# An eighteenth weight slot, taken from GpSimd's descriptor scratch, and a turned ring in layer 1

## The chip, the cores and the metric

The kernel runs on one core of one Trainium2 chip. The metric is the device time of one execution in microseconds, as the median of several runs. TensorE multiplies (its weight loads are listed apart as PEld), VectorE (DVE), ScalarE (ACT) and GpSimd (POOL) do the rest, and SyncE (SP) issues nearly all weight loads. Sixteen DMA engines move the data between memory and the on-chip rows of 128 partitions. They are fed by three queues that matter here: q1 is SyncE's, q10 is ScalarE's, q0 is GpSimd's, whose descriptors GpSimd writes by itself into a scratch area in each partition.

## What is computed

One step of a two-layer encoder trunk on 512 new frames and 32 further frames of a running stream, model width 1024, all in float32.

```python
for i in range(DEPTH):                       # two layers
    hp_n = rms_norm(hp, norm_mix[i]); hs_n = rms_norm(hs, norm_mix[i])
    if i % N_MIXERS == 0:                    # layer 0: sliding window attention, 16 heads, 4 kv heads
        yp, kp_, vp_ = mixer_a_prompt(hp_n, w_a_qkv[j], b_a_qkv[j], a_sinks[j], w_a_o[j])
    else:                                    # layer 1: differential attention, 8 heads
        yp, kp_, vp_ = mixer_b_prompt(hp_n, w_b_qkv[j], b_lambda[j], b_subln[j], w_b_o[j], lam_init)
    hp = hp + yp
    hp = hp + hier_moe(rms_norm(hp, norm_ffn[i]), ...)
y_prompt = rms_norm(hp, norm_final)

# hier_moe: top-1 of 4 groups, then top-2 of its 8 experts
a = jnp.einsum('nd,edf->nef', x, w_gate[g])
u = jnp.einsum('nd,edf->nef', x, w_up[g])
hh = jax.nn.silu(a) * u * gate[:, g, :, None]
y = y + jnp.einsum('nef,efd->nd', hh, w_down[g])
```

Each expert has three matrices (gate, up, down) of 1 MB each, and there are 32 experts in each layer, so an expert stage reads 96 MB.

## The kernel before

The program goes through four stages: mixer A, the expert stage of layer 0, mixer B, the expert stage of layer 1. Frames lie in five tiles, four of 128 rows and one of 32 (tile 4).

**Weights and slots.** Every weight is loaded in pieces of 1 MB, one piece to a slot of 2048 floats in each partition (`SLOT`). There are 17 slots for the expert weights, and they are named after what else lies there: R0 to R5 are the ring for the mixers' weights (`A_RING`, `B_RING`, lines 172 and 173), F0 to F6 hold keys, values, tables and the transposed input during attention, N0 and N1 the rows of the norm, X0 and X1 the router's input. `MOE_SLOTS` (line 175) lists them in the order in which the expert weights take them, round and round. `weight_loads` gives each weight its slot, and the loop under it notes who held it before (`BEFORE`).

**The order on SyncE.** SyncE issues all loads in the order of their use: the 10 of mixer A, 96 of layer 0's experts, 16 of mixer B (q, k and v of four pairs of heads, then the four pieces of the output matrix), 96 of layer 1's experts. Before each, `load_after_owner` (line 475) waits until the last user of what the slot held is done. The first turn of the expert weights waits with `vacant` for the attention's data instead. As the queue is in order, a load whose slot is not free holds up all that follow it.

**Overfull experts.** An expert takes up to 64 rows (`CAP`). If one has more, its weights are loaded once more after expert 29 (`OV_AFTER`), into three slots side by side (`ovw`), which the numbering of the stream leaves out (`expert_stream`). With these inputs that happens once, in layer 1 (line 488).

**One expert.** GpSimd gathers its rows (line 611), TensorE turns them (L1955), multiplies by gate and up (L1970, L1971), ScalarE and VectorE make the product, TensorE turns it (L1976) and multiplies by down (L1982, L1983), VectorE copies the result (L1407), GpSimd scatters it to a scratch tensor in memory (L617). When all scatters of a layer have landed, ScalarE's queue reads them back tile by tile (L927, semaphores `tile_in`), VectorE adds them to the residual (L1506, L1507), and the next norm begins.

**Space.** `area` is one array that fills the partition beside a few small ones. GpSimd's scratch for descriptors has the program's default size of 16384 bytes a partition.

Of the kernel before, what the change touches and what calls it, by code (L numbers as in the profile page):

```python
# [31 lines left out]
NT = 5  # L32
# [23 lines left out]
SLOT = 2048  # L56
XG = 4
OV_AFTER = 29
# [88 lines left out]
def out_items(layer):  # L147
# [10 lines left out]
    if layer == 0:  # L158
# [9 lines left out]
            for layer in range(2)]  # L168
# [1 line left out]


A_RING = ["R0", "R1", "R2", "R3", "R4", "R5"]
B_RING = ["R4", "R5", "R0", "R1", "R2", "R3"]
FREED = ["F5", "F6", "F0", "F1", "F2", "F3", "F4"]
MOE_SLOTS = [["R4", "R5"] + FREED + ["R0", "R1", "R2", "R3", "N0", "N1", "X0", "X1"],
             ["R2", "R3"] + FREED + ["R4", "R5", "R0", "R1", "N0", "N1", "X0", "X1"]]
NSLOT = len(MOE_SLOTS[0])


def expert_stream(e, j):  # L180
    return 3 * (e + (e > OV_AFTER)) + j


def weight_loads():
    loads = [("a", x, i) for x, n in (("k", 1), ("v", 1), ("q", 4), ("o", 4)) for i in range(n)]
    loads = [(key, A_RING[i % 6]) for i, key in enumerate(loads)]
    moe = [[(("e", layer, e, j), MOE_SLOTS[layer][expert_stream(e, j) % NSLOT]) for e in range(NE) for j in range(3)]
           for layer in range(2)]
    b = [("b", x, p) for p in range(PAIRS) for x in "kvq"] + [("b", "o", s) for s in range(4)]
    b = [(key, B_RING[i % 6]) for i, key in enumerate(b)]  # L190
    return loads, moe, b


A_LOADS, MOE_LOADS, B_LOADS = weight_loads()
WHERE, BEFORE = {}, {}
turns, owner = {}, {}
for weight, slot_name in A_LOADS + MOE_LOADS[0] + B_LOADS + MOE_LOADS[1]:
# [1 line left out]
    WHERE[weight] = slot_name, 16 * turns[slot_name]  # L199
    BEFORE[weight] = owner.get(slot_name)  # L200
    owner[slot_name] = weight
assert [MOE_SLOTS[layer][(3 * (OV_AFTER + 1) + j) % NSLOT] for layer in range(2) for j in range(3)] == ["F1", "F2", "F3"] * 2


def build(nc, I, O):
    ctx = ExitStack()
    with ctx:
        program(nc, ctx, I, O)


def program(nc, ctx, I, O):
    def sb(name, shape, dt=F32):
        return ctx.enter_context(nc.sbuf_tensor(name, shape, dt))

    def sem(name):
        return ctx.enter_context(nc.semaphore(name))
# [13 lines left out]
    R_X = M0 + 3248  # L230
    R_N = R_X + KD * N
    R_R = R_N + 4 * D
    R_F = R_R + 6 * SLOT
    AREA = R_F + 5 * SLOT + KD * N
    area = sb("area", [P, AREA])

    def part(at, *shape):
        n = int(np.prod(shape))
        v = area[:, at:at + n]
        if len(shape) == 2:  # L240
            v = v.rearrange("p (a b) -> p a b", b=shape[1])
        if len(shape) == 3:
            v = v.rearrange("p (a b c) -> p a b c", b=shape[1], c=shape[2])
        return v

    slot_at = {f"R{i}": R_R + SLOT * i for i in range(6)}
    slot_at.update({f"F{i}": R_F + SLOT * i for i in range(7)})
    slot_at.update({f"N{i}": R_N + SLOT * i for i in range(2)})
    slot_at.update({f"X{i}": R_X + SLOT * i for i in range(2)})


    oT = part(R_X, KD, N)
    xTn = [part(R_F + 5 * SLOT, KD, N), oT, part(R_F + 5 * SLOT, KD, N), oT]

# [7 lines left out]
    dist_a = part(R_X + 3328, 2 * P)  # L262
    kTa = part(R_F, A_KV, SEQ + WINDOW + DEC)
    tabA = part(R_F + A_KV * (SEQ + WINDOW + DEC), A_HEADS, 2 * P)
    R_VA = R_F + A_KV * (SEQ + WINDOW + DEC) + A_HEADS * 2 * P
    va = part(R_VA, 6, AKV)
# [29 lines left out]
    hts = [part(M1 + 1536 + 128 * i, 2, CAP) for i in range(2)]  # L296
    yout = [part(M1 + 1792 + 512 * i, OUT_HALF) for i in range(3)]
    assert M1 + 1792 + 3 * 512 <= M0
    ovw = part(R_F + SLOT, 3, SLOT)
    y2b = [part(2 * D * i, 2, D) for i in range(3)] + [part(R_X + 2 * D * i, 2, D) for i in range(2)]  # L300
    assert 6 * D <= M0 and 4 * D <= KD * N

# [39 lines left out]
    tile_in = [sem(f"tile_in{i}") for i in range(NT)]  # L342
# [11 lines left out]
    hid_moe = sem("hid_moe")  # L354
    k_out = sem("k_out")
    kb_out, vb_out = [sem(f"kb_out{i}") for i in range(2)], [sem(f"vb_out{i}") for i in range(2)]
    pool_own, dve_own, act_own = sem("pool_own"), sem("dve_own"), sem("act_own")
    q_mm, q_act, q_dve = sem("q_mm"), sem("q_act"), sem("q_dve")
    kv_mm, kv_sb, k_flip, k_sb = sem("kv_mm"), sem("kv_sb"), sem("k_flip"), sem("k_sb")
    pos_mm, pos_dve, pos_act = sem("pos_mm"), sem("pos_dve"), sem("pos_act")  # L360
# [27 lines left out]
    def wait_apart(eng, s, value):  # L388

        eng.wait_ge(s, value)  # L390
        eng.sem_inc(passed, 1)

    def weights(key):
        name, value = WHERE[key]
        return part(slot_at[name], SLOT), w_ready[name], value

    def last_use(key):

        kind, x, i = key[0], key[1], key[2]
        if kind == "e":  # L400
            return (d_mm if key[3] == 2 else gu_mm), NE * x + i + 1
        if x == "o":
            return o_mm, OUT_BASE["ab".index(kind) + 1]
        if kind == "a":
            return (q_mm, 4 * i + 4) if x == "q" else (kv_mm, NT)
        reads = {"k": "K KS", "v": "V KS", "q": "Q"}[x].split()
        return pos_mm, 1 + max(n for n, s in enumerate(POS) if s.pair == i and s.main in reads)
# [41 lines left out]
    @block.sync  # L449
    def _(sp):  # L450
        def rows8(w, lo, hi):
            return w[:, lo:hi].rearrange("(p k) f -> p k f", k=KD)

        def rows128(w, lo, hi):
            return w[:, lo:hi].rearrange("(k p) f -> p k f", p=P)

        gate = [I["w_gate"][l].rearrange("g e (p k) f -> (g e) p k f", k=KD) for l in range(2)]
        up = [I["w_up"][l].rearrange("g e (p k) f -> (g e) p k f", k=KD) for l in range(2)]
        down = [I["w_down"][l].rearrange("g e (c p) d -> (g e) p c d", p=P) for l in range(2)]

        def source(key):
            kind, x, i = key[0], key[1], key[2]
            if kind == "e":
                return (gate, up, down)[key[3]][x][i]
            if x == "o":
                return rows128(I[f"w_{kind}_o"][0], F * i, F * i + F)
            at_col = {"aq": 0, "ak": AQ, "av": AQ + AKV, "bq": 0, "bk": D, "bv": 2 * D}[kind + x] + F * i
            return rows8(I[f"w_{kind}_qkv"][0], at_col, at_col + F)

        def load(key):  # L470
            dst, landed, _ = weights(key)
            src = source(key)
            sp.dma_start(dst.rearrange("p (k f) -> p k f", f=src.shape[-1]), src).then_inc(landed, 16)  # L473

        def load_after_owner(key):
            if BEFORE[key] is not None:
                sp.wait_ge(*last_use(BEFORE[key]))
            load(key)

        def moe_loads(layer):  # L480
            s = ov[layer]

            def overfull_weights(o):
                wait_apart(sp, s["pick"], o + 1)
                e = sp.value_load(ov_u[0:1, 0:1], min_val=0, max_val=NE - 1)
                for j, w in enumerate((gate, up, down)):
                    src = w[layer][bass.ds(e, 1)].rearrange("o p k f -> p (o k) f")
                    sp.dma_start(ovw[:, j, :].rearrange("p (k f) -> p k f", f=src.shape[-1]), src) \
                      .then_inc(s["w"], 16)

            for n, (key, name) in enumerate(MOE_LOADS[layer]):
                if key[2:] == (OV_AFTER + 1, 0):
                    for j in range(3):
                        e, w = divmod(expert_stream(OV_AFTER + 1, 0) - 3 + j - NSLOT, 3)
                        sp.wait_ge(*last_use(("e", layer, e, w)))
                    sp.wait_ge(s["count"], 1)
                    extra = sp.value_load(ov_i[0:1, layer:layer + 1], min_val=0, max_val=MAX_EXTRA)
                    with sp.If(extra > 0):
                        overfull_weights(0)
                free = vacant(layer, name) if expert_stream(*key[2:]) < NSLOT else None  # L500
                if free is None:
                    load_after_owner(key)
                else:
                    for signal in free:
                        sp.wait_ge(*signal)
                    load(key)

            with sp.If(extra > 1):
                with sp.Fori(1, extra) as o:
                    overfull_weights(o)  # L510

        for n, (key, name) in enumerate(A_LOADS):
            if n == 0:
                sp.wait_ge(tile_in[0], 16)
            if n == 2:
                sp.wait_ge(tile_in[2], 16)
            load_after_owner(key)
        moe_loads(0)
        for key, name in B_LOADS:
            load_after_owner(key)  # L520
        moe_loads(1)

# [250 lines left out]

    @block.scalar
    def _(act):
        own = Link(act_own)

        def square(n, i):
            t = TILES[n][i]
            r = ROWS[t]  # L780
# [90 lines left out]
        for step in range(UNITS):  # L871
# [3 lines left out]
            j, i = divmod(step, NT)  # L875
# [1384 lines left out]
```

## Time and profile before

| | us |
|---|---|
| median of 3 runs | 1256.02 |
| lowest and highest | 1254.98, 1256.83 |
| the profiled execution | 1257.34 |
| its span, first to last instruction | 1255.6 |

| Engine | busy us | share |
|---|---|---|
| TensorE matmul | 1060.9 | 84% |
| TensorE weight load | 754.9 | 60% |
| VectorE | 419.2 | 33% |
| ScalarE | 220.3 | 18% |
| GpSimd | 282.6 | 23% |

The mean granted clock of TensorE is 0.932. The stages stand in time like this: mixer A until about 250 us, the experts of layer 0 until 536, mixer B from 558 to about 920, the experts of layer 1 until 1214, and then the last norm and the outputs. A busy share over the whole span hides this: what a change in a stage is worth is read from that stage's own waits.

### The profile page before, as it was taken

To read this page: it belongs to the slowest core of one execution; us is meant where nothing else is said; L and a number is where in the kernel's file an instruction comes from. 1 tells how busy PE (TensorE), PEld (TensorE's weight loads), DVE (VectorE), ACT (ScalarE), POOL (GpSimd) and SP (SyncE) were. 2 spreads that over 40 slices of the span, in tenths; PEclk is the share of its full clock that TensorE was granted. 3 is DMA by queue.
4 is the path that set the end of the run, shared out by engine and by line. 5 is a ranking of instruction groups with operands and counts; after the bars stand their busy time and mean duration, and the time that the engine had idled before them with its cause. 6 is when DMAs were issued, how large, how long until landed. Compare 5 with 4: busy or idle time off the path is not lost.

```text
span 1255.6 us, 17940 instructions
## 1 busy us (share of the span) xinstructions
PE 1060.9 (84%) x6864; PEld 754.9 (60%) x6864; DVE 419.2 (33%) x1340; ACT 220.3 (18%) x687; POOL 282.6 (23%) x445
## 2 busy tenths in 40 slices
PE   5999999949988887819999999999959997888850
PEld 4877778935545544518677686867845554554520
DVE  2234554322222222243243424345542322321225
ACT  2134442110000000011123322323310000000001
POOL 2512231012321212131021222221211222222113
PEclk9999999969999999959999999999969999898885
DMA  9211124199999999980322203060378999999943
GB/s 313 71 63 34 54 83 189 38 334 342 371 380 382 388 381 373 346 308 15 102 77 79 67 29 117 27 252 1 122 271 311 379 374 383 375 384 382 387 155 148
DMA packets 81239, 279.00 MB, mean 222 GB/s; under 512 B 10958, under 2 KB 37662, under 8 KB 63424
## 3 DMA queue, kind: packets, MB, share of 16 engines
q1 hardware_dynamic: 63440, 231.75, 50.1%
q0 software_dynamic: 15840, 34.92, 8.6%
q10 hardware_dynamic: 1872, 11.14, 2.4%
q8 instruction: 58, 0.95, 0.3%
q14 instruction: 29, 0.24, 0.1%
HBM read 265.50 MB, written 28.70 MB: 234 GB/s over the span
## 4 chain that ended last, share of the span: by engine, by line
PE 61%; DMA 26%; SPq 3%; DVE 3%; issue 2%; ACT 2%; POOL 1%; POOLq 0%; ACTq 0%; DVEq 0%
PE ps L1689 20%; DMA area<-in_w_up 18%; PE ps L1970 11%; PE ps L1681 10%; PE ps L1982 4%; SPq L473 3%; PE ps L1955 2%; DMA area<-in_w_down 2%; PE ps L1697 2%; PE ps L2162 2%; DMA hn_scratch<-area 1%; PE ps L1853 1%; PE ps L2128 1%; DMA area<-hn_scratch,idx_i 1%; PE ps L1868 1%
## 5 line engine op out<-in xcount | busy, mean ns | idle before, releaser
L1970 PE MATMUL ps<-area 128*64 128x256 f32 x1040 | 265.2, 413 | 60.4 <-DMA area<-in_w_up 52.6
L1689 PE MATMUL ps<-area 128*128 128x256 f32 x1152 | 267.0, 385 | 5.6 <-DMA area<-in_w_a_qkv 3.1
L1971 PE MATMUL ps<-area 128*64 128x256 f32 x1040 | 265.9, 414 | 0.0
L1689 PEld LDWEIGHTS ps<-area 128*128 128x128 f32 x1152 | 215.8, 192 | 36.7 <-issue 8.0
L1970 PEld LDWEIGHTS ps<-area 128*64 128x64 f32 x1040 | 149.7, 149 | 134.9 <-issue 76.9
L617 POOL DMA_INDIRECT y_scratch<-area,idx_i x64 | 64.8, 1013 | 401.7 <-DVE area L1407 396.9
L1971 PEld LDWEIGHTS ps<-area 128*64 128x64 f32 x1040 | 149.6, 149 | 0.0
L1982 PE MATMUL ps<-area 128*64 128x512 f32 x260 | 125.4, 604 | 1.1 <-DVE area L1400 0.8
L1983 PE MATMUL ps<-area 128*64 128x512 f32 x260 | 125.4, 604 | 0.0
L1681 PE MATMUL ps<-area 128*128 128x272 f32 x512 | 123.2, 395 | 0.0
L1392 DVE TENSOR_TENSOR area<-area,ps 64x256 f32<-64x256 f32 x64 | 27.2, 425 | 283.0 <-ACT area L903 283.0
L903 ACT ACTIVATE area<-ps 64x256 f32<-64x256 f32 x64 | 24.1, 376 | 508.6 <-PE ps L1971 508.6
L1681 PEld LDWEIGHTS ps<-area 128*128 128x128 f32 x512 | 95.0, 190 | 18.9 <-issue 0.6
L865 ACT ACTIVATE area<-area,small 128x256 f32<-128x256 f32 (+5 forms) x160 | 80.2, 502 | 87.1 <-DVE small L1157 87.1
L1955 PEld LDWEIGHTS ps<-cst,area 64*128 64x128 f32 x512 | 61.3, 200 | 45.6 <-issue 34.5
L1955 PE MATMUL ps<-cst,area 64*128 64x64 f32 x512 | 70.2, 278 | 21.5 <-DMA area<-hn_scratch,idx_i 21.5
L1150 DVE CUSTOM_DVE_ANT_0 area<-ps,area 128x256 f32<-128x256 f32 (+5 forms) x160 | 59.1, 423 | 44.9 <-PE ps L1853 25.2
L611 POOL DMA_INDIRECT area<-hn_scratch,idx_i x64 | 60.8, 949 | 47.9 <-issue 29.4
L729 POOL TENSOR_SCALAR area<-area,small 32x288 f32<-32x288 f32 (+4 forms) x40 | 20.6, 524 | 166.3 <-DVE small L1577 166.3
L1982 PEld LDWEIGHTS ps<-area 128*64 128x64 f32 x260 | 30.4, 136 | 42.9 <-issue 37.1
L1386 DVE TENSOR_TENSOR area<-ps,gT 128x512 f32<-128x512 f32 x65 | 44.9, 691 | 31.7 <-PE ps L1955 28.3
L602 POOL TENSOR_SCALAR area<-area,small 128x256 f32<-128x256 f32 (+2 forms) x80 | 33.9, 442 | 93.9 <-DVE small L1185 93.9
(218 smaller groups left out, 1059.0 us busy)
## 6 DMA issues: line engine op xcount, KB each, us to landing
area<-in_w_gate SPq DMA_DIRECT2D x65, 1024.0 KB, 26.9
area<-in_w_up SPq DMA_DIRECT2D x65, 1024.0 KB, 26.5
area<-in_w_down SPq DMA_DIRECT2D x65, 1024.0 KB, 26.8
area<-in_w_b_qkv SPq DMA_DIRECT2D x12, 1024.0 KB, 9.6
area<-y_scratch ACTq DMA_DIRECT2D x8, 1024.0 KB, 10.5
area<-in_w_a_qkv SPq DMA_DIRECT2D x6, 1024.0 KB, 13.2
out<-area POOLq DMA_DIRECT2D x12, 512.0 KB, 3.5
area<-in_w_a_o SPq DMA_DIRECT2D x4, 1024.0 KB, 5.3
```

Source lines behind the costliest of these rows:

```text
L611: nc.gpsimd.indirect_dma_start(xg[e % XG][0:CAP, :], None, hn_dram, bass.IndirectOffsetOnAxis(ap=idx_i[0:CAP, 1, e:e + 1], axis=0), bounds ...
L617: nc.gpsimd.indirect_dma_start(y2_dram, bass.IndirectOffsetOnAxis(ap=idx_i[:, 0, e:e + 1], axis=0), yout[e % 2], None, bounds_check=4 * N ...
L865: ins = nc.scalar.activation(E[:r, g, 0:nk], E[:r, g, 0:nk], ACT.Exp, bias=sm[:r, 4 + g:5 + g], scale=SCALE, accum_out=sm[:r, 8 + g:9 + g])
L1150: ins = nc.vector.tensor_tensor_reduce(out=E[:r, g, 0:nk], in0=ps[:r, b, c:c + nk], in1=tab(j, g)[:r, tc:tc + nk], scale=1.0, scalar=-3e38 ...
L1386: return nc.vector.tensor_tensor(x, ps[:, bank, :].rearrange("p (k c) -> p k c", c=CAP), gT[:, layer, :].unsqueeze(2).broadcast_to([P, KD, ...
L1681: ins = nc.tensor.matmul(ps[:, bank, 0:HALF_N], w[:, k, m * P:m * P + P], x[:, k, HALF_N * h:HALF_N * h + HALF_N], start=k == 0, stop=k == ...
L1689: ins = nc.tensor.matmul(ps[:r, bank, at_col:at_col + F], x[:, k, COL[t]:COL[t] + r], w[:, k, :], start=k == k0, stop=k == k1 - 1)
L1955: ins = nc.tensor.transpose(ps[:, 2 + b, k * CAP:k * CAP + CAP], x[:, k, :], ident[0:CAP, 0:CAP])
L1970: nc.tensor.matmul(ps[0:CAP, bank, 0:F], x[:, k, :], wg[:, k, :], start=k == 0, stop=k == KD - 1)
L1971: ins = nc.tensor.matmul(ps[CAP:P, bank, 0:F], x[:, k, :], wu[:, k, :], start=k == 0, stop=k == KD - 1)
L1982: nc.tensor.matmul(ps[0:CAP, bank, :], ht[:, c, :], wd[:, c, 0:OUT_HALF], start=c == 0, stop=c == 1)
L1983: ins = nc.tensor.matmul(ps[CAP:P, bank, :], ht[:, c, :], wd[:, c, OUT_HALF:D], start=c == 0, stop=c == 1)
```

## The change

1. The program is made with a scratch of 4096 bytes a partition for GpSimd's descriptors in place of 16384. Of the 12288 bytes, `area` takes 8192 for one further slot, S0, right behind R5.
2. S0 becomes the third entry of the list of slots, which now has 18 entries and is the same for both layers. The order of mixer B's ring changes so that it begins with R0.
3. The overfull expert's weights go to R4, R5 and S0 in place of F1, F2 and F3.
4. Before the fifth load of mixer B, SyncE waits until the y rows of the last tile of layer 0 have landed (`tile_in[NT - 1]` at 32).
5. A semaphore and a helper of ScalarE that nothing used are left out.

```diff
 A_RING = ["R0", "R1", "R2", "R3", "R4", "R5"]
-B_RING = ["R4", "R5", "R0", "R1", "R2", "R3"]
+B_RING = ["R0", "R1", "R2", "R3", "R4", "R5"]
 FREED = ["F5", "F6", "F0", "F1", "F2", "F3", "F4"]
-MOE_SLOTS = [["R4", "R5"] + FREED + ["R0", "R1", "R2", "R3", "N0", "N1", "X0", "X1"],
-             ["R2", "R3"] + FREED + ["R4", "R5", "R0", "R1", "N0", "N1", "X0", "X1"]]
+MOE_SLOTS = [["R4", "R5", "S0"] + FREED + ["R0", "R1", "R2", "R3", "N0", "N1", "X0", "X1"]] * 2
...
-    R_F = R_R + 6 * SLOT
+    R_S = R_R + 6 * SLOT
+    R_F = R_S + SLOT
...
+    slot_at["S0"] = R_S
...
-    ovw = part(R_F + SLOT, 3, SLOT)
+    ovw = part(R_R + 4 * SLOT, 3, SLOT)
...
-        for key, name in B_LOADS:
+        for n, (key, name) in enumerate(B_LOADS):
+            if n == 4:
+                sp.wait_ge(tile_in[NT - 1], 32)
             load_after_owner(key)
...
-    nc = bacc.Bacc("TRN2", target_bir_lowering=False, num_devices=1)
+    nc = bacc.Bacc("TRN2", target_bir_lowering=False, num_devices=1, dynamic_dma_scratch_size=4096)
```

## Rows read from the trace of the kernel before

**Rows 1.** The page, part 2: busy tenths of the DMA engines in 40 slices

```profile
DMA  9211124199999999980322203060378999999943
```

**Rows 2.** Sums by stretch: stretch, length, engines' busy us, clock, DMA share, GB/s

```profile
280.00:290.00 10.00, 9.82 (x78) 5.92 (x80) 2.33 (x6) 0.38 (x1) 1.03 (x1) 1.00 0.71 264
...
350.00:530.00 180.00, 147.78 (x1010) 90.58 (x1008) 40.07 (x80) 7.52 (x20) 38.02 (x39) 0.93 1.01 376
...
1040.00:1190.00 150.00, 124.27 (x822) 74.93 (x819) 37.98 (x92) 6.02 (x16) 30.45 (x32) 0.89 1.02 383
```

**Rows 3.** Waits of TensorE, 272 to 540 us: total us, times, longest

```profile
PE ps L1970 <- DMA area<-in_w_up: 32.2, 18, 3.5
```

**Rows 4.** Waits of TensorE, 938 to 1216 us

```profile
PE ps L1970 <- DMA area<-in_w_up: 20.4, 10, 4.4
...
PE ps L1970 <- DMA area<-in_w_down: 1.5, 1, 1.5
```

**Rows 5.** The page, part 6: DMA issues, KB each, us from issue to landing

```profile
area<-in_w_gate SPq DMA_DIRECT2D x65, 1024.0 KB, 26.9
...
area<-in_w_b_qkv SPq DMA_DIRECT2D x12, 1024.0 KB, 9.6
```

**Rows 6.** Timeline of SyncE before the experts of layer 0: start, us, what

```profile
154.79 0.41 SPq L473 DMA_DIRECT2D area<-in_w_gate  x1
204.08 0.33 SPq L473 DMA_DIRECT2D area<-in_w_up  x1
...
249.55 0.33 SPq L473 DMA_DIRECT2D area<-in_w_gate  x1
...
278.42 0.38 SPq L473 DMA_DIRECT2D area<-in_w_down  x1
```

**Rows 7.** Timeline of SyncE before the experts of layer 1

```profile
822.02 0.88 SPq L473 DMA_DIRECT2D area<-in_w_gate  x1
830.87 0.33 SPq L473 DMA_DIRECT2D area<-in_w_up  x1
```

**Rows 8.** The chain that ended last, end of layer 1: start, us, what

```profile
1160.87 26.97 DMA area<-in_w_down
...
1214.38 2.71 DMA y_scratch<-area,idx_i
1217.17 6.01 DMA area<-y_scratch
```

**Rows 9.** Timeline of TensorE: the expert before the overfull one; idle before, and releaser

```profile
1175.26 0.40 PE L1970 MATMUL ps<-area 128*64 128x256 f32 x1 [0.72 <-DMA area<-in_w_up]
```

**Rows 10.** Timeline of SyncE, end of layer 0

```profile
508.22 30.49 SPq L473 DMA_DIRECT2D area<-in_w_b_qkv  x6
```

**Rows 11.** The chain that ended last, end of layer 0

```profile
536.56 6.26 DMA y_scratch<-area,idx_i
...
542.91 8.35 DMA area<-y_scratch
```

**Rows 12.** DMA queues, 543 to 552 us: packets, MB, share of 16 engines

```profile
q10 hardware_dynamic: 235, 1.79, 49.0%
...
q1 hardware_dynamic: 605, 0.62, 21.2%
```

**Rows 13.** Line 473 from 501.5 us on: the last expert weight of layer 0

```profile
L473 SPq DMA_DIRECT2D area<-in_w_down x1: 6536/6536/6536, 501.5 to 501.5; - x1
...
DMA to landing us min/median/max: 27.9/27.9/27.9
```

**Rows 14.** Timeline of TensorE: its first products for head pair 1

```profile
618.49 3.72 PE L1689 MATMUL ps<-area 128*128 128x256 f32 x16
```

**Rows 15.** Line 617, all scatters: ns min/median/max, first and last start

```profile
L617 POOL DMA_INDIRECT y_scratch<-area,idx_i x64: 982/1015/1034, 288.8 to 1214.4; - x64
...
DMA to landing us min/median/max: 2.3/7.1/8.5
```

**Rows 16.** Timeline of GpSimd, end of layer 0, last of seven

```profile
540.29 0.63 POOL L683 DMA_DIRECT2D area<-in_dist_b  x1
```

More of the change, by code:

```diff
@@ L201 @@
     owner[slot_name] = weight
-assert [MOE_SLOTS[layer][(3 * (OV_AFTER + 1) + j) % NSLOT] for layer in range(2) for j in range(3)] == ["F1", "F2", "F3"] * 2
+assert [MOE_SLOTS[layer][(3 * (OV_AFTER + 1) + j) % NSLOT] for layer in range(2) for j in range(3)] == ["R4", "R5", "S0"] * 2
 def build(nc, I, O):
@@ L356, in program @@
     kb_out, vb_out = [sem(f"kb_out{i}") for i in range(2)], [sem(f"vb_out{i}") for i in range(2)]
-    pool_own, dve_own, act_own = sem("pool_own"), sem("dve_own"), sem("act_own")
+    pool_own, dve_own = sem("pool_own"), sem("dve_own")
     q_mm, q_act, q_dve = sem("q_mm"), sem("q_act"), sem("q_dve")
@@ L775, in _ @@
     def _(act):
-        own = Link(act_own)
         def square(n, i):
```

## The prediction

> **What bounds the kernel now.** I read the page's second part first, for which slices are held by which resource, then the sums by stretch, then who waited for whom on TensorE, then the chain at the end of each layer's expert stage, and last SyncE's own timeline, because SyncE issues every weight load in a fixed order. In the slices the reader is to see two long runs in which the DMA line stands at 9 [rows 1]: these are the two expert stages. By stretch, the DMA share is 1.01 and 1.02 at 376 and 383 GB/s from 350 to 530 us and from 1040 to 1190 us, while TensorE is busy for 148 of 180 and 124 of 150 us [rows 2]. TensorE's idle time there is put down to weights that had not landed: 32.2 us in 18 waits in layer 0 [rows 3], 20.4 us in 10 waits in layer 1 and another 1.5 us on the overfull expert's down weight [rows 4]. So both expert stages end when the stream of weights ends. A load counts 1024 KB, and from issue to landing it takes 26.9 us at the median [rows 5]; so some ten loads stand queued, and SyncE runs far ahead of TensorE. Before each of these stages there is plenty of DMA time with nothing in it (the 0s and 2s of the DMA line), because all slots that are free are full. What matters for the end of a stage is how many bytes have landed when the stream becomes unbroken.
>
> **The eighteenth slot, layer 0.** Loads now start as slots fall free, in batches: R4 first, then three up to 154.79 (R5, F5, F6), five from 204.08 (F0 to F4), four from 249.55 (R0 to R3), four when the norm's and the router's rows are out (N0 to X1), and the first reuse at 278.42 [rows 6], which has the last of the second batch and the first of each later one. With S0 third in the list, the batch at 154 has four loads (R5, S0, F5, F6), and every later batch has as many as before, at the same times, because the same events free the same slots. Each is one load further on in the stream. The added load follows 154.79, some 50 us before the next batch, and finds a 1 and a 2 in the DMA line [rows 1]. The stall after it does not go: from 280 to 290 us the DMA share is 0.71 [rows 2], since R4, R5 and then the next slots wait for TensorE's first two experts (278.42 is the first), and those are not earlier. From there the stream is unbroken to its end, and it has one load less to bring: 1.049 MB at 376 GB/s is **2.8 us**. Ends: 0, if TensorE came to be the bound, and 2.8. I take 2.8, since the waits that would have to be used up first are 32.2 us.
>
> **Layer 1.** The same count: four loads up to 822.02 (R2, R3, F5, F6) become five (R4, R5, S0, F5, F6), and the three from 830.87 are as before [rows 7]. The ring order of mixer B is only turned, so that each of its weights still takes the slot of the weight six before it, and R4, R5 are now the ones that its last two hold. The stream ends earlier by 1.049 MB at 383 GB/s, **2.7 us**. Here the end is tighter. The chain passes the overfull expert's down weight, which lands at 1160.87 + 26.97 = 1187.84 [rows 8], and TensorE waited for that for 1.5 us only [rows 4]. But the expert ahead of it itself began at 1175.26 on a landing [rows 9], so it moves with the stream. Ends 0 and 2.7; I take 2.7.
>
> **Between the layers.** The overfull weights move from F1 to F3 to R4, R5 and S0, so the new code gives mixer B's first four loads R0 to R3 and holds the fifth and sixth (v and q of head pair 1) until the last y rows of layer 0 are in. Before, six loads go out in the 30.49 us from 508.22, until 538.7 [rows 10], beside the last scatter and the y rows. What this costs is seen by setting the two ends side by side: from the issue of the last scatter to the landing of the first y rows it is 6.26 + 8.35 us plus the issue in layer 0 [rows 11] and 2.71 + 6.01 us in layer 1, where no such loads run [rows 8]. The difference, 5.9 us, is what all traffic beside it costs. While the first y rows were under way (543 to 552 us), SyncE's queue moved 0.62 MB beside 1.79 MB of ACT's [rows 12]. In the new order the stream and its four loads end earlier: the last expert weight lands at about 526.6 (issued at 501.5, landed 27.9 later [rows 13], less 2.8), the four loads follow at about 3 us each, so until 539, against a scatter issued at 533.8 (536.56 less 2.8). So the scatter gains about 1 us of its 3.6 us excess, and the y rows the 0.62 MB, at 385 GB/s 1.6 us, together **2.5 us**. Ends: 0 and 5.9.
> The Trainium skill (DMA: Bandwidth & Descriptors, Queues, rings and completion order) says that each DMA engine takes turns between its queues packet by packet. ACT's packets are 7.6 KB and SyncE's 1.0 KB here (bytes by packets), so by that rule SyncE's two loads would take an eighth as much as the y rows, 0.2 MB or 0.6 us, and the sum would be 1 us smaller (1249.0 us, between the forecast and rival B). The trace has 0.62 MB against 1.79 MB, a third, and I go by that.
>
> **The wait added on SyncE** (on the y rows of tile 4) has queued behind it v and q of pair 1, then k, v and q of pair 2. The y rows of tile 4 are in soon after the first ones (551.3 less 2.8 and 2.5), by about 557, and mixer B's weights land after 9.6 us at the median [rows 5], so v and q are there by some 570. TensorE reaches pair 1's k at 618.49 [rows 14], and v and q only after that; k of pair 2 has to wait for the last use of pair 0's k in both kernels, which is later than 557. A cover of some 50 us; cost nothing. The unused link of ScalarE and the shifted addresses are no instructions.
>
> **The smaller scratch.** GpSimd issues 64 gathers and 64 scatters of 1.0 us each, which land after 7.1 us at the median and 8.5 at most (scatters [rows 15]). One scatter and one gather go per expert of some 8 us, so two to four are in flight, and the densest stretch (two scatters and five loads, the last at 540.29 [rows 16]) has at most eight. The durations from the first to the last scatter, 0.982 to 1.034 us, do not grow with what has gone before. No row shows a full ring. Bounds: nothing, and a wait for the landing of the DMA before, 7.1 us for each of about seven issues on the chain. I take nothing, as a quarter of the space for at most eight DMAs is nearer to the rows than a wait for the previous one.
> The skill gives the scratch as 16 KiB a partition (SBUF: State Buffer, SBUF size: 192, 224, or 256?) and nine 16-byte descriptors per engine for a 1 MiB transfer (DMA: Bandwidth & Descriptors, The descriptor swizzle). An estimate from both is 256 descriptors or 28 such transfers in what is left. No run here shows that number.
>
> **The sum.** 2.8 + 2.5 + 2.7 = 8.0 us. The profiled execution took 1257.34 us (span 1255.6 and 1.7 around it), so it would be 1249.3; it lies 1.3 over the median of 1256.02, so the median becomes **1248.0 us**.
>
> **Rivals.**
> *A, layer 1 keeps its end.* The overfull expert needs a gather as well, and TensorE's mean clock is down to 0.89 there [rows 2], so its own chain may end the stage. For it: only 1.5 us of wait on the last weight [rows 4]. Against: expert 29 began on a landing. 2.8 + 2.5 gives 1250.7. 0.17.
> *B, no relief between the layers.* The scatter and y rows are slowed by GpSimd's own five loads [rows 16], which stay, and only the streams gain: 5.5 us, 1250.5. For it: 0.62 MB is little in 9 us. 0.15; a relief of half the size (1249.2) lies between B and the forecast, and in the forecast's chance.
> *C, full relief.* The whole 5.9 us goes: 11.4 us, 1244.6. Against: four loads still run into the scatter. 0.06.
> *D, slower: the descriptor ring fills.* Its place is GpSimd's issue. On the chain are the last row write and first gather and the last scatter of each layer and the last output, seven issues. The gain of 8.0 us is gone from 1.14 us more for each, that is if an issue of 1.0 us becomes one of 2.1. With two more us for each it is +14 - 8 = +6, 1262. In the expert loop it would have to pass (8 - 2)/2 = 3 us an issue before GpSimd paces the stage; a wait for the landing before would do it, 2 x 8.1 us an expert against 8, and cost hundreds of us. 0.06.
> *E, it does not do what it says.* The added load lands early, but the DMA stall at 280 and 950 us grows by as much, so the streams end as now, and the relief is small: within 2.5 us of 1256. For it: SyncE's order is fixed. Against: no event that frees a slot moves later. 0.06.
>
> **Chances and range.** The forecast has 0.50. 0.2% is 2.5 us, about what a measurement of this kernel can tell from no change: faster by more than that 0.87 (forecast, A to C, less 0.01), same 0.07, slower 0.06. The range takes in C, A and B with their spread and leaves out D and E: 1244.3 to 1252.8.
>
> **What would show it.** After: the batch before 160 us has one load more; the stall near 285 us stays; the last landing of layer 0's stream and the last scatter (now 536.56) come 2.5 to 3 us earlier; from last scatter to first combine 12 us in place of 14.7; mixer B the same length; layer 1's last scatter (1214.38) 8 us earlier; the weight waits on TensorE less by about 2.8 us each; GpSimd's issues at 1.015 us. Wrong: a scatter issue above 1.1 us, TensorE waiting for v or q of pair 1, or a layer's weight waits unchanged.

## The result and the profile after

| | before | changed |
|---|---|---|
| median of 4 runs, us | 1256.22 | 1241.22 |
| lowest and highest | 1254.98, 1256.83 | 1240.47, 1244.46 |
| the profiled execution | 1257.34 | 1244.46 |
| its span | 1255.6 | 1242.7 |
| granted clock of TensorE | 0.932 | 0.935 |

The ratio is 0.9882, with a 95% interval from 0.9868 to 0.9896, so the change takes off 14.8 us (13.1 to 16.6). A later set of six runs gave 1242.80 against 1256.42, ratio 0.9899 (0.9882 to 0.9915), 12.7 us less (10.7 to 14.8). Fast executions alone count here and below: one of the eight of the kernel with all but the slot took 2654.79 us and is left out. I had predicted 1248.0, in a range from 1244.3 to 1252.8: the direction was right, the gain was nearly twice the forecast and lay outside the range.

Line numbers of the new kernel are one higher (L1971 is L1970 of before), GpSimd's gather L614 and its scatter L620. First, SyncE's timeline (start, us, engine line op, tiles): the second batch, which has four loads now, and what follows the batch at 248 us.

```profile
152.19 0.34 SPq L474 DMA_DIRECT2D area<-in_w_up  x1
152.57 0.43 SPq L474 DMA_DIRECT2D area<-in_w_down  x1
153.12 0.40 SPq L474 DMA_DIRECT2D area<-in_w_gate  x1
153.62 0.71 SPq L474 DMA_DIRECT2D area<-in_w_up  x1
...
247.89 0.33 SPq L474 DMA_DIRECT2D area<-in_w_up  x1
...
261.33 0.38 SPq L474 DMA_DIRECT2D area<-in_w_down  x1
...
279.45 0.33 SPq L474 DMA_DIRECT2D area<-in_w_gate  x1
```

The added load is there, in a batch that is over long before the next one. But the first reuse comes 31.56 us after the batch at 248 us (279.45 - 247.89), where it came 28.87 us after it before (278.42 - 249.55, [rows 6]). Most of that difference is between executions: over all profiles the reuse comes 30.1 us after the batch at the mean of seven with 17 slots (28.9 to 30.9) and 30.9 at the mean of five with 18 (29.5 to 31.6). So the stall stayed, as I had said, and by these means it grew by some 0.8 us. The sum of the stretch from 280 to 290 us (columns as in [rows 2]) shows it in the changed kernel, with a share of 0.65 and 228 GB/s against 0.71 and 264:

```profile
280.00:290.00 10.00, 9.46 (x76) 5.73 (x77) 3.18 (x7) 0.38 (x1) 0.13 (x1) 1.00 0.65 228
```

TensorE's waits on weights from 272 to 540 us (total, times, longest), against 32.2 in [rows 3]:

```profile
PE ps L1971 <- DMA area<-in_w_up: 29.2, 17, 4.2
```

and from 938 to 1216 us, against 20.4 and 1.5 in [rows 4]:

```profile
PE ps L1971 <- DMA area<-in_w_up: 19.3, 10, 4.0
...
PE ps L1971 <- DMA area<-in_w_down: 1.6, 1, 1.6
```

The chain that ended last (start, us, what), first at the end of layer 0, then at the end of layer 1 and at the very end:

```profile
534.17 5.22 DMA y_scratch<-area,idx_i
...
539.47 7.28 DMA area<-y_scratch
```

```profile
1208.43 2.82 DMA y_scratch<-area,idx_i
1211.34 6.00 DMA area<-y_scratch
...
1238.44 0.52 POOL out L549
```

From the last scatter's issue to the landing of the first y rows it is 12.6 us (534.17 to 546.75) where it was 14.7 in [rows 11]. Layer 1's last scatter is 5.95 us earlier than in [rows 8] (1208.43 against 1214.38), and the last piece of the chain stands 5.9 us earlier too. Yet the span is 12.9 us shorter. Some 7 us therefore went after everything that the chain of waits shows. The view of the program's last line has them (op, times, ns min/median/max, first and last start). Of before, where it was there to be read:

```profile
L207 DVEq DRAIN  x1: 1303/1303/1303, 1242.7 to 1242.7; - x1
...
L207 POOLq DRAIN  x1: 8650/8650/8650, 1246.7 to 1246.7; - x1
...
L207 SPq EVENT_SEMAPHORE  x1: 17/17/17, 1255.5 to 1255.5; - x1
```

and of the changed kernel:

```profile
L206 POOLq DRAIN  x1: 1627/1627/1627, 1240.8 to 1240.8; - x1
```

Near the end of each engine's part of the program stands an instruction DRAIN, and SyncE's last instruction comes behind the longest of them. VectorE's takes 1.3 us and is over before GpSimd's begins. GpSimd's took 8.65 us at the end of the path in the kernel before, and 1.63 us in the changed one: **7.0 us**. It is not spent on data under way: in every profile the last output has landed 0.2 us before this drain begins (1246.50 and 1246.68 in the kernel before, 1240.64 and 1240.82 in the changed one). No work of GpSimd had been taken away, only space; it issues 198 DMAs in both kernels. The experiments ask if this is so, and where the rest came from.

### The profile page after: what moved, and what is told of

Its sections match the earlier page's. It is cut to its first block, busy times and chain, and to the rows that moved or that the text cites. A ratio compares the mean times of both kernels' runs of the same rounds, so it can differ in the third digit from the quotient of the medians.

```text
span 1242.7 us, 17941 instructions
## 1 busy us (share of the span) xinstructions
PE 1061.1 (85%) x6864; PEld 756.9 (61%) x6864; DVE 419.0 (34%) x1340; ACT 220.1 (18%) x687; POOL 281.5 (23%) x445
## 4 chain that ended last, share of the span: by engine, by line
PE 63%; DMA 24%; SPq 5%; DVE 3%; issue 2%; ACT 2%; POOL 1%; POOLq 0%; ACTq 0%; DVEq 0%
PE ps L1690 20%; DMA area<-in_w_up 16%; PE ps L1971 11%; PE ps L1682 10%; PE ps L1983 4%; SPq L474 4%; PE ps L1956 2%; DMA area<-in_w_down 2%; PE ps L1698 2%; PE ps L2163 2%; DMA hn_scratch<-area 2%; DMA area<-hn_scratch,idx_i 1%; PE ps L1854 1%; PE ps L2129 1%; PE ps L1869 1%
## 5 line engine op out<-in xcount | busy, mean ns | idle before, releaser
L1971 PE MATMUL ps<-area 128*64 128x256 f32 x1040 | 265.1, 413 | 56.2 <-DMA area<-in_w_up 48.5
L1971 PEld LDWEIGHTS ps<-area 128*64 128x64 f32 x1040 | 149.6, 149 | 129.8 <-issue 68.0
L620 POOL DMA_INDIRECT y_scratch<-area,idx_i x64 | 64.7, 1010 | 398.2 <-DVE area L1408 362.1
L1151 DVE CUSTOM_DVE_ANT_0 area<-ps,area 128x256 f32<-128x256 f32 (+5 forms) x160 | 59.1, 423 | 44.9 <-PE ps L1854 25.2
L614 POOL DMA_INDIRECT area<-hn_scratch,idx_i x64 | 60.6, 947 | 49.7 <-issue 30.3
L732 POOL TENSOR_SCALAR area<-area,small 32x288 f32<-32x288 f32 (+4 forms) x40 | 20.5, 521 | 166.4 <-DVE small L1578 166.4
L1387 DVE TENSOR_TENSOR area<-ps,gT 128x512 f32<-128x512 f32 x65 | 44.9, 691 | 33.2 <-PE ps L1956 30.1
## 6 DMA issues: line engine op xcount, KB each, us to landing
area<-in_w_a_qkv SPq DMA_DIRECT2D x6, 1024.0 KB, 13.1
```

Source lines behind the costliest of these rows:

```text
L614: nc.gpsimd.indirect_dma_start(xg[e % XG][0:CAP, :], None, hn_dram, bass.IndirectOffsetOnAxis(ap=idx_i[0:CAP, 1, e:e + 1], axis=0), bounds ...
L620: nc.gpsimd.indirect_dma_start(y2_dram, bass.IndirectOffsetOnAxis(ap=idx_i[:, 0, e:e + 1], axis=0), yout[e % 2], None, bounds_check=4 * N ...
L1151: ins = nc.vector.tensor_tensor_reduce(out=E[:r, g, 0:nk], in0=ps[:r, b, c:c + nk], in1=tab(j, g)[:r, tc:tc + nk], scale=1.0, scalar=-3e38 ...
L1971: nc.tensor.matmul(ps[0:CAP, bank, 0:F], x[:, k, :], wg[:, k, :], start=k == 0, stop=k == KD - 1)
```

## The experiments

Theory R (reclaiming): the drain's length hangs on the scratch, alone worth 7 us. Its rival T: the space isn't the cause, and the whole gain comes from the slot and the hold. The parts were tried one at a time.

**The scratch alone.** The kernel before with

```diff
+    nc = bacc.Bacc("TRN2", target_bir_lowering=False, num_devices=1, dynamic_dma_scratch_size=4096)
```

> The kernel before with 4096 bytes of scratch in place of 16384, and nothing else: no slot S0, the old rings. In the trace of before, GpSimd's last drain takes 8.65 us of the span, in that of after 1.63 us. Theory R (the drain pays for each GpSimd DMA whose descriptors are still kept, and a small ring keeps few): the drain falls to about 1.6 us, everything ahead of it stays where it was, time -7.0 us, 1249.2. Rival S (the short drain comes from the slot or the new order of the loads, not from the scratch): drain 8.6 us, time within 1 us of before. Rival F (a small ring costs GpSimd on each issue, which the slot's gain has hidden): scatters above the 1.015 us of before, less than 7 us gained.

Measured: 1249.40 against 1257.21, ratio 0.9942 (0.9921 to 0.9962), 7.3 us less (4.8 to 9.9). Its last drain:

```profile
L207 POOLq DRAIN  x1: 1627/1627/1627, 1245.1 to 1245.1; - x1
```

Theory R holds, T falls: half of the change's gain comes with 17 slots and no word changed in the order of work. Scatters take 1.012 us at the median (1.015 in [rows 15]), so the small ring costs GpSimd nothing at the issue.

**The hold alone.** The kernel before with

```diff
+        for n, (key, name) in enumerate(B_LOADS):
+            if n == 4:
+                sp.wait_ge(tile_in[NT - 1], 32)
```

> The kernel before with the new wait alone: v and q of head pair 1 go out only when the y rows of tile 4 are in; 17 slots, 16384 bytes. Theory (relief between the layers): from the issue of the last scatter of layer 0 to the first combine 12.2 to 12.9 us in place of 14.7, time -2 us, 1254.2. Rival B of the prediction (no relief, GpSimd's own loads slow it): 14.7 us again, time unchanged. The drain at the end stays at 8.6 us in both.

Measured: 1254.25, ratio 0.9983 (0.9970 to 0.9995), 2.1 us less (0.6 to 3.8). In its chain the last scatter and the y rows are

```profile
535.59 5.62 DMA y_scratch<-area,idx_i
...
541.29 6.70 DMA area<-y_scratch
```

which is 12.4 us in all where [rows 11] give 14.7. Over all profiles, from the last scatter to the first y rows it is 14.3 to 16.2 us in the five without the hold (four of them below 15), and 11.9 to 12.7 in the eight with it and 17 or 18 slots. The means of those below 15 and of the eight are 2.4 us apart (14.7 and 12.3); with the fifth, of 16.2 us, it would be 2.7.

**Both without the slot.** Scratch of 4096 and the hold, on the kernel before.

```diff
+            if n == 4:
+                sp.wait_ge(tile_in[NT - 1], 32)
...
+    nc = bacc.Bacc("TRN2", target_bir_lowering=False, num_devices=1, dynamic_dma_scratch_size=4096)
```

> The kernel before with 4096 bytes of scratch and with the new wait ahead of the fifth load of mixer B, but 17 slots: all of the change but the slot. The prediction's slot is worth 5.5 us, the first runs' sum for the scratch and the wait is 7.3 + 2.1. Theory: the parts add up, so this is 9.4 us under before (1246.8 against 1256.2) and 5.5 us over the changed kernel. Rival A (layer 1 keeps its end with the slot): only 3 us over the changed kernel.

Measured: 1248.57 against 1255.86, ratio 0.9947 (0.9928 to 0.9966), so 6.7 us less (4.3 to 9.0). The 9.4 us of the two parts added up lie just over that interval, and within it when the parts' own intervals are counted; by its profile the two terms are there (drain 1.63 us, 11.9 us from last scatter to first y rows). What the slot adds to this kernel is 6.0 us by the ratios of this run and the later set (0.9947 and 0.9899), 8.2 by the first set (0.9882). Each ratio is known to about 2 us, so these times fit the forecast of 5.5, but don't settle the slot's worth to within 2 us.

**The slot in layer 0 only.** The changed kernel, where layer 1 keeps 17 slots and its overfull weights go to F1 to F3:

```diff
-MOE_SLOTS = [["R4", "R5", "S0"] + FREED + ["R0", "R1", "R2", "R3", "N0", "N1", "X0", "X1"]] * 2
+MOE_SLOTS = [["R4", "R5"] + s + FREED + ["R0", "R1", "R2", "R3", "N0", "N1", "X0", "X1"] for s in (["S0"], [])]
```

> The changed kernel with S0 in layer 0 alone; layer 1's experts have the 17 slots of before, and its overfull weights F1 to F3. Theory (2.7 us for each layer): 2.7 us over the changed kernel, the last expert weight of layer 1 lands 2.7 us later after the stage's first load, and so does the last scatter. Rival A: the landing is later, the last scatter is not (under 1 us), time within 1 us of the changed kernel.

Measured: 1245.16, ratio 0.9912 (0.9890 to 0.9934): between the kernel without a slot (0.9947) and the whole change (0.9882 and 0.9899), about half way. That is what a gain in each layer would give, but the interval overlaps those of its neighbours, so the time alone doesn't show it. By its profile, layer 1's last weight lands 381.9 us after the layer's first load and the last scatter goes out 393.7 us after it, as with 17 slots throughout (381.0 to 382.7, and 393.0 to 394.1); with S0 in layer 1 it is 379.7 to 380.7 and 389.4 to 393.3. So the stream of layer 1 gains by the slot in each profile, and its last scatter in the mean; rival A, that layer 1 keeps its end, doesn't hold as a whole.

**How the drain depends on the scratch.** Three more sizes, all with the work otherwise as it was: 8192 and 2048 in the changed kernel, 12288 in the kernel before, and the changed kernel once more beside them.

```diff
-    nc = bacc.Bacc("TRN2", target_bir_lowering=False, num_devices=1, dynamic_dma_scratch_size=4096)
+    nc = bacc.Bacc("TRN2", target_bir_lowering=False, num_devices=1, dynamic_dma_scratch_size=8192)
```

> The changed kernel with 8192 bytes of scratch in place of 4096. Theory R: the last drain lies between that of 4096 and that of 16384 bytes, about 3.5 us, so the time is 1243 to 1244, 2 us over the changed kernel; everything ahead of the drain as there. Rival S: drain 1.6 us, time as the changed kernel's 1241.2.

```diff
-    nc = bacc.Bacc("TRN2", target_bir_lowering=False, num_devices=1)
+    nc = bacc.Bacc("TRN2", target_bir_lowering=False, num_devices=1, dynamic_dma_scratch_size=12288)
```

> The kernel before with 12288 bytes of scratch, for the length of the last drain alone. 4096 and 8192 bytes both gave 1.63 us, 16384 gives 8.65. If what is kept is given back only when the scratch is full, and then all of it at once, 12288 bytes must give a drain that depends on where in the run it was last full: anything from 1 to 6 us, with 8.65 only if it is never full. If instead the scratch keeps a fixed number of bytes' worth of DMAs, the drain lies on a line between 1.63 at 8192 and 8.65 at 16384, so about 5 us. Rival: a step, 1.63 or 8.65.

```diff
-    nc = bacc.Bacc("TRN2", target_bir_lowering=False, num_devices=1, dynamic_dma_scratch_size=4096)
+    nc = bacc.Bacc("TRN2", target_bir_lowering=False, num_devices=1, dynamic_dma_scratch_size=2048)
```

> The changed kernel with a scratch of 2048 bytes in place of 4096. If the last drain is a price by size, it falls from 1.63 us to about 0.8; if by steps, as 8192 and 4096 had the same 1.63, it is 1.6 or 0.7 (the run with 1408 bytes and 19 slots had 0.73). Scatter issues stay at 1.015 us in any case, and the time is that of the changed kernel, less 0 to 1 us. If a ring this small fills, an issue in the loop grows above 1.1 us and the time rises.

> The changed kernel once more, beside the two above: 1241 to 1245 us, last drain 1.63 us.

Measured: with 8192 bytes 1244.57, ratio 0.9901 (0.9884 to 0.9919); with 12288 1256.29 in one run; with 2048 1244.85, 0.9908 (0.9893 to 0.9924), beside 1242.80 for the changed kernel again. The last drains of 8192, 12288 and 2048 bytes:

```profile
L206 POOLq DRAIN  x1: 1627/1627/1627, 1241.2 to 1241.2; - x1
```

```profile
L207 POOLq DRAIN  x1: 7180/7180/7180, 1247.1 to 1247.1; - x1
```

```profile
L206 POOLq DRAIN  x1: 1300/1300/1300, 1236.5 to 1236.5; - x1
```

I had expected a price by size, about 3.5 us at 8192. It is 8.65, 7.18, 1.63, 1.63, 1.30 us for 16384, 12288, 8192, 4096, 2048 bytes: nearly flat up to 8192, with a large step between that and 12288. (The one run with 12288 bytes is read for its drain only.) Of a ring smaller than 4096 the time shows nothing (2048 came out 2 us above the changed kernel, within the two intervals), and half of the default gives the same drain as a quarter, 7 us less than before. What the step is made of isn't settled by these.

**How it depends on what was issued.** If the price is for DMAs that were issued and not yet cleared away, a drain earlier in the program should take most of it off the end. In the kernel before (16384 bytes), a drain in the loop of layer 1, where GpSimd has idle time:

```diff
                 scatter(e)
+                if layer and e == 24:
+                    nc.gpsimd.drain()
```

> The kernel before with one more drain on GpSimd after the scatter of expert 24 of layer 1, where GpSimd has idle time between its issues; 17 slots, 16384 bytes. Theory R: the drain in the loop takes 8 us or more there (it waits for the scatter in flight and goes through what is kept), the last one falls to about 1 us because only some 20 DMAs are left to it, time -6 to -7 us, 1249 to 1250. Rival (the last drain waits for something at the end of the program, such as the outputs' writes): last drain 8.6 us again, time unchanged or slower by what the drain in the loop delays the gathers.

Measured: 1250.53, ratio 0.9949 (0.9932 to 0.9966), 6.4 us less. The drain in its loop, and the one at its end:

```profile
L652 POOLq DRAIN  x1: 10349/10349/10349, 1150.7 to 1150.7; - x1
```

```profile
L207 POOLq DRAIN  x1: 1536/1536/1536, 1247.9 to 1247.9; - x1
```

The scratch is that of before, and the price has left the end all the same. GpSimd started nothing for 10 us where the new drain stands, as its timeline shows (last bracket: idle before, releaser), between the scatter of that expert and its next gather:

```profile
1150.89 1.01 POOL L617 DMA_INDIRECT y_scratch<-area,idx_i  x1 [8.58 <-DVE area L1409]
1161.88 0.94 POOL L611 DMA_INDIRECT area<-hn_scratch,idx_i  x1 [9.98 <-issue]
```

and hardly anyone was late for it. Gathers run four experts ahead: TensorE waited 0.3 us for one between 1150 and 1180 us. The next scatter went out right behind that gather, late by a few microseconds, and the ones after it waited for VectorE's results again. Layer 1 took 394.1 us from its first load to its last scatter, inside the spread of the profiles with 17 slots. The same drain after expert 8 instead:

```diff
-                if layer and e == 24:
+                if layer and e == 8:
```

> The kernel before (scratch of 16384 bytes) with a drain of GpSimd after the scatter of expert 8 of layer 1 in place of expert 24. The last drain took 1.54 us with 19 DMAs issued since the one before, and 8.65 us with all 198. If its price grows with that number in a line, 0.04 us each, it is 2.8 us here with some 51 left; if it is a step, it is 1.5 or 8.6. The time is some 6 us below the kernel before in the first case.

```profile
L207 POOLq DRAIN  x1: 4149/4149/4149, 1247.2 to 1247.2; - x1
```

It grows with the number issued since the last drain, but not in the line I had drawn: 1.54 us for 19 DMAs, 4.15 for 51 (2.8 expected), 8.65 for all 198. The one run took 1253.38 against 1256.57 beside it. So with the full scratch the last drain is the longer, the more has been issued since the one before. One reading is that a small ring is cleared on the way, each time it comes round, and leaves little for the end; no run shows that, and by which rule the length goes with size and number stays open.

**What another order gives.** With 19 slots the overfull expert's three would not lie side by side in the list as it stands, so that I had to move R0 behind N1. That kernel (scratch 1408, S0 and S1, overfull weights in N0, N1 and R0, the hold ahead of mixer B's fourth load in place of the fifth, and one semaphore of GpSimd's loads shared with another):

```diff
-B_RING = ["R0", "R1", "R2", "R3", "R4", "R5"]
+B_RING = ["R1", "R2", "R3", "R0", "R4", "R5"]
...
-MOE_SLOTS = [["R4", "R5", "S0"] + FREED + ["R0", "R1", "R2", "R3", "N0", "N1", "X0", "X1"]] * 2
+MOE_SLOTS = [["R4", "R5", "S0", "S1"] + FREED + ["R1", "R2", "R3", "N0", "N1", "R0", "X0", "X1"]] * 2
```

> A further slot S1 beside S0: 19 slots, with 1408 bytes of scratch, the overfull weights in N0, N1 and R0, R0 last but two in the list, mixer B's ring R1, R2, R3, R0, R4, R5 with the wait ahead of its fourth load. Theory: another 2.7 us in each layer and a little more relief, -5 us against the changed kernel, 1236; last drain 1.6 us or less. Rival (a ring this small is full at times, so GpSimd's issues wait): scatters above 1.015 us or issues of the five loads after layer 0 and of mixer B's rows above 1 us, and a time over 1238.

Measured: 1227.86, ratio 0.9772 (0.9748 to 0.9796), 28.6 us below the kernel before and 14 to 15 below the changed one (by its two ratios), where I had expected 5. To tell the order from the slot, the order alone on the changed kernel (18 slots, 4096 bytes):

```diff
-B_RING = ["R0", "R1", "R2", "R3", "R4", "R5"]
+B_RING = ["R1", "R2", "R3", "R0", "R4", "R5"]
...
-MOE_SLOTS = [["R4", "R5", "S0"] + FREED + ["R0", "R1", "R2", "R3", "N0", "N1", "X0", "X1"]] * 2
+MOE_SLOTS = [["R4", "R5", "S0"] + FREED + ["R1", "R2", "R3", "N0", "N1", "R0", "X0", "X1"]] * 2
```

> The changed kernel (18 slots, scratch 4096) with slot R0 moved behind N1 in the list of slots, so that the batch at 248 us has three loads and the next one five; mixer B's ring begins with R1 to fit. Theory P (part of what the kernel with 19 slots gained is this order): the first gather of layer 0 lands 21.2 us after that batch in place of 23.2 and TensorE starts earlier, both stages end earlier, 2 to 6 us in all. Theory Q (it was the slot alone): the same time as the changed kernel within 1 us.

Measured: 1237.44, ratio 0.9852 (0.9834 to 0.9870), against 1242.80 for the changed kernel beside it: 5.4 us for the place of one name in a list. Theory P held, in its middle. SyncE's timeline of this kernel:

```profile
248.06 0.33 SPq L474 DMA_DIRECT2D area<-in_w_up  x1
...
260.09 0.33 SPq L474 DMA_DIRECT2D area<-in_w_up  x1
...
275.84 0.33 SPq L474 DMA_DIRECT2D area<-in_w_gate  x1
```

The batch at 248 us has three loads here. The next batch waits for a DMA of the norm's rows that is issued right after that batch; the rows that TensorE's first expert gathers are read from the same scratch tensor. The next batch comes 12.03 us after the first (13.44 in the changed kernel), and the first gather lands 20.5 us after it (23.2). The first reuse then comes 27.8 us after (31.56), so the whole stage starts earlier, and layer 0's last weight lands 275.2 us after that batch in place of 278.5. All of these lie outside the spread of the five profiles with 18 slots in the old order (12.9 to 14.4, 22.3 to 23.4, 29.5 to 31.6 and 277.4 to 279.9 us), and layer 1's stream is shorter as well, 377.6 us against 379.7 to 380.7. Its waits on `in_w_up` are 25.9 us against 29.2:

```profile
PE ps L1971 <- DMA area<-in_w_up: 25.9, 13, 4.5
```

The rest of the 19-slot kernel's lead, 9.6 us by the two medians (1237.44 and 1227.86), is in its profile: layer 0's stream 2.2 us shorter (273.0), layer 1's 4.7 (372.9 against 377.6), between the layers 1.9 (10.3 us from last scatter to first y rows), the drain 0.9. To the last scatter, which is what the path goes by, the two stages are 2.6 and 3.3 us shorter. Which of the second slot, its batch and the earlier hold brings which part was not taken apart.

## Why the prediction was wrong

**What bounds the kernel.** Right: one load less in the unbroken part shortens each stage. In layer 0 TensorE's waits on `in_w_up` went down with it, from 32.2 to 33.9 us in the seven profiles with 17 slots to 27.6 to 29.3 in the five with 18. In layer 1 they show nothing: 20.4 and 19.3 us in the two profiles above, but 17.9 to 26.0 over the eight with 17 slots there and 18.8 to 20.7 over the four with 18.

**The smaller scratch, "I take nothing".** This is the step that failed, and by its size it is all of the miss: 7.0 us against 6.8 (14.8 measured, 8.0 forecast). I asked only what a smaller ring might cost at each issue, and bounded it between nothing and 7.1 us an issue. Nothing in the trace excluded a gain; I had not looked for one. Two numbers that stood before me asked for it: the chain of waits ended at 1244.82, the span at 1255.6. The chain's last row in the kernel before:

```profile
1244.30 0.52 POOL out L546
```

Nearly 11 us at the end of the path had no owner in my account, and the prediction doesn't mention them; 8.65 of them are the drain. The views by busy time and the chain don't list a drain, since it belongs to the instructions that are not counted as busy; the view of the program's last line does. Sizes that answer: 8.65 us before, 1.63 after, and 7.3 us for the scratch alone. With that term the sum would have been 8.0 + 7.0 = 15.0 us, against 14.8 measured.

**That sum would have been right partly by luck.** For the streams I use the time from the batch at 248 us (or from layer 1's first expert load) to the landing of the last weight, since the start of that batch itself moves by up to 4 us from one profile to the next.

| | 17 slots | 18 slots | difference | forecast |
|---|---|---|---|---|
| layer 0, batch to last weight | 280.6 (7 profiles) | 278.3 (5) | 2.3 | 2.8 |
| layer 0, batch to last scatter | 288.0 (7) | 286.0 (5) | 2.0 | 2.8 |
| layer 1, first load to last weight | 382.0 (8) | 380.2 (4) | 1.8 | 2.7 |
| layer 1, first load to last scatter | 393.5 (8) | 391.4 (4) | 2.1 | 2.7 |

With 2.4 between the layers (2.5 forecast) and 7.0 for the drain (0 forecast) the terms are 2.0 + 2.1 + 2.4 + 7.0 = 13.5 us, inside both measured intervals (13.1 to 16.6, and 10.7 to 14.8). So 15.0, near as it is to the first measurement, would have held two slot terms that are too large by these means. How much of that is luck isn't settled: the mean of layer 1's last scatter isn't sure (see below), and the times of the kernel with all but the slot leave room for the full 5.5 us.

**The eighteenth slot, layer 0** (2.8) and **layer 1** (2.7): the mechanism right, the size too large by the profiles. The assumption that failed is "TensorE's first two experts are not earlier", read as if they were not later either. The first gather lands 22.9 us after the batch at the mean of the five profiles with the slot and 22.1 without it, and in layer 1 118.3 us after the first load against 117.4: some 0.9 us later in both (from 22.3 to 23.4 against 21.5 to 22.9, which overlap, and from 117.9 to 118.6 against 116.8 to 118.0, which hardly do). 0.9 us off 2.8 and 2.7 leaves 1.9 and 1.8, near the 2.3 and 1.8 by which the streams are shorter. The run with R0 moved shows how sharply this start answers to what is queued ahead of the norm's rows: 2.7 us between two profiles for one load. Why the same four loads stand in its way for 0.9 us more with the slot isn't shown; I leave it open.

**Layer 1's end.** Rival A had its reasons, and it decides from one execution to the next. In the profile of the change, 28.0 us pass from the landing of the overfull expert's last weight to the last scatter. The sums of that stretch in before, in the change and in the change once more:

```profile
1187.80:1214.40 26.60, 21.74 (x142) 11.60 (x142) 5.41 (x11) 1.13 (x3) 3.00 (x4) 0.94 0.37 149
```

```profile
1180.40:1208.40 28.00, 23.17 (x142) 12.38 (x142) 5.41 (x11) 1.12 (x3) 2.98 (x3) 0.89 0.36 145
```

```profile
1182.10:1207.40 25.30, 20.28 (x142) 10.65 (x142) 5.70 (x12) 1.13 (x3) 3.22 (x5) 1.00 0.39 158
```

The granted clock is 0.94, 0.89 and 1.00, and the stretch takes 26.6, 28.0 and 25.3 us: at the end of layer 1 TensorE's own work sets the pace, and the three lengths differ by as much as a slot is worth (2.7 us), the longest at the lowest clock. It is so in all fourteen profiles, whatever the kernel: 25.2 and 25.3 us where the granted clock was 1.00, 26.5 to 27.6 where it was 0.91 to 0.94, 27.8 to 28.5 where it was 0.88 to 0.90. Of the last weight's 2.7 us (382.7 to 380.0) the profile of the change kept 1.2 us at the last scatter (393.7 to 392.5); the later one, at the full clock, had 4.3 (389.4). So a single profile can't settle the last scatter's term, and the mean of four, 2.1, is less sure than the others.

**Between the layers** (2.5): right in size, 2.4 by the profiles and 2.1 in time for the hold alone. My reason in parts held as well: SyncE's queue moved 0.05 MB from 536 to 552 us, in the place of 0.62 MB in nine of those microseconds [rows 12]. The scatter's landing took 5.22 us in place of 6.26, the 1 us that I had given it, and the y rows 7.28 in place of 8.35, 1.1 us where I had 1.6. The smaller sum that stood beside mine, with 1.5 us of relief, fits less well, though the hold's own interval (0.6 to 3.8) doesn't exclude it. Rivals B (no relief) and C (all of 5.9 us) fall.

**The wait on SyncE, costed at nothing**: right. SyncE stood in it for 27.0 us, and v and q of pair 1 landed at 562.1 and 565.0, far ahead of head pair 1's first product (618.49 before, [rows 14]).

```profile
SPq L474 <- DMA area<-y_scratch: 27.0, 1, 27.0
```

**Rival D, the ring fills**: not seen down to 1408 bytes. The scatters of the change:

```profile
L620 POOL DMA_INDIRECT y_scratch<-area,idx_i x64: 982/1012/1031, 289.9 to 1208.4; - x64
```

**Rival E** falls with each landmark that moved.

**What I said would show it.** One load more in the batch, the stall, 12 us between scatter and combine, and issues at 1.015 us: all came. Layer 0's last scatter was 2.4 us earlier, for 2.5 to 3. Not so: layer 1's last scatter was to be 8 us earlier and was 5.95; the weight waits in layer 1 fell by 1.1, not 2.8, which is less than their spread. By my own list, unchanged weight waits in a layer would have been a sign of being wrong; they were too unsteady a sign for 2.8 us.

## What to carry to other kernels

Account for the whole span before summing a change, from the last output to the last instruction: what no view by busy time lists (a drain, a barrier) is path like all else, and here it held half of the gain. When a resource is made smaller, ask what its size costs now as well as what it may cost then, and let the bound go below zero unless a row forbids it. And when a stage's start hangs on a short DMA behind a batch of large ones, look first at what is queued ahead of it: moving one load from before it to after it brought 5.4 us in two layers, about what the slot brought (4.1 us by the landmarks, 6 to 8 by the times).

## What was not expected of the hardware

- GpSimd's closing drain took 8.65 us with a 16384-byte scratch and 198 DMAs issued, 7.18 with 12288, 1.63 with 8192 and with 4096, 1.30 with 2048 and 0.73 with 1408. With the scratch at 16384 and a drain on the way it took 4.15 us after 51 further DMAs and 1.54 after 19.
- A drain in the middle of the expert loop held GpSimd for 10.3 us (9.3 in the run with expert 8) and delayed nothing that ended the stage.
- GpSimd's closing drain begins after the last output has landed, so its length is not a wait for data.
- A DMA ring of a twelfth of the default space (1408 bytes) kept the issue of an indirect scatter at 1.012 us, with a gather and a scatter for every expert.
